# Modulation units in pairs, with the first two dense units accumulated between them

## The reference, cut to what matters

```
m  = silu(cond) @ w_ada + b_ada          # 6 * 2048 wide, for two conditions
sh1, sc1, g1, sh2, sc2, g2 = split(m, 6)
h  = rmsnorm(x, n1g) * (1 + sc1) + sh1   # pre-norm and modulation
u  = h @ w_in                            # one wide input projection: GLU | q | k | v | gates
```

## Time and profile before

| | |
|---|---|
| median of 3 runs | 3283.35 us (3283.23 to 3284.37) |
| profiled execution, its own time | 3287.09 us |
| profiled execution, span of the trace | 3285.5 us |
| granted TensorE clock, mean | 0.965 |
| TensorE matmul busy | 3072.2 us, 94% of the span |
| VectorE busy | 1935.6 us, 59% |
| ScalarE busy | 1391.3 us, 42% |
| read from HBM | 681.60 MB |

### The profile page before, as it was taken

One profiled execution on the slowest core, in us unless ns is written; L12 is line 12 of the kernel. 1 busy time (PEld: TensorE's weight loads), 2 busy tenths in 40 slices (PEclk: granted clock), 3 DMA queues, 4 the chain that ended last, 5 costly groups with the idle time before them and its releaser, 6 DMA issues.

```text
span 3285.5 us, 52731 instructions
## 1 busy us (share of the span) xinstructions
PE 3072.2 (94%) x20582; PEld 2612.3 (80%) x20582; DVE 1935.6 (59%) x1988; ACT 1391.3 (42%) x1669; POOL 278.1 (8%) x438
## 2 busy tenths in 40 slices
PE   5599999999999899989999999599999999999995
PEld 4499999999989898979999999466666666666663
DVE  4323332136556465657325333599999989999894
ACT  2311111124333342433312122277777777777774
POOL 0011110001100100111001111100000000000000
PEclk7699999999999999999999999799999999999997
DMA  8533332224534444454334533599999999999994
GB/s 356 208 113 118 119 123 100 77 89 156 191 140 153 183 157 178 162 188 143 126 133 169 165 125 118 213 345 390 388 390 379 374 382 390 385 383 378 374 388 136
DMA packets 123892, 745.97 MB, mean 227 GB/s; under 512 B 16592, under 2 KB 26896, under 8 KB 43968
## 3 DMA queue, kind: packets, MB, share of 16 engines
q1 hardware_dynamic: 96368, 631.28, 49.8%
q0 software_dynamic: 27376, 112.60, 11.0%
HBM read 681.60 MB, written 55.66 MB: 224 GB/s over the span
## 4 chain that ended last, share of the span: by engine, by line
PE 76%; DVE 9%; issue 5%; ACT 3%; DMA 2%; DVEq 0%; SPq 0%; POOL 0%; ACTq 0%; POOLq 0%
PE pu L849 22%; PE pu L593 15%; PE pu L594 15%; PE pu L595 15%; DVE elo L1652 4%; PE pt L697 2%; PE pt L573 2%; ACT ehi L1152 2%; DVE xe L1664 1%; PE pt L685 1%; PE ps L667 1%; DVE wlo L1229 1%; PE ps L675 1%; ACT whi L882 1%; DMA att<-att 1%
## 5 line engine op out<-in xcount | busy, mean ns | idle before, releaser
L593 PE MATMUL pu<-hhi,whi 128*128 128x320 f32 x3328 | 1048.0, 315 | 49.8 <-DVE wlo L1229 32.1
L594 PE MATMUL pu<-hlo,whi 128*128 128x320 f32 x3328 | 1032.8, 310 | 1.4 <-issue 1.4
L595 PE MATMUL pu<-hhi,wlo 128*128 128x320 f32 x3328 | 1032.4, 310 | 0.0
L1652 DVE TENSOR_TENSOR elo<-ering,ehi 128x2048 fp32r<-128x2048 f32 x384 | 874.9, 2288 | 107.1 <-ACT ehi L1152 103.9
L1152 ACT CAST ehi<-ering 128x2048 fp32r<-128x2048 f32 x384 | 731.5, 1912 | 238.3 <-PE pu L849 238.1
L593 PEld LDWEIGHTS pu<-hhi,whi 128*128 128x128 f32 x3328 | 629.5, 189 | 51.9 <-issue 46.3
L594 PEld LDWEIGHTS pu<-hlo,whi 128*128 128x128 f32 x3328 | 629.3, 189 | 3.9 <-issue 2.1
L595 PEld LDWEIGHTS pu<-hhi,wlo 128*128 128x128 f32 x3328 | 628.6, 189 | 0.0
L1229 DVE TENSOR_TENSOR wlo<-raw,whi 128x2048 fp32r<-128x2048 f32 x112 | 256.6, 2291 | 291.5 <-ACT whi L882 290.7
L882 ACT CAST whi<-raw 128x2048 fp32r<-128x2048 f32 x112 | 213.0, 1902 | 503.4 <-PE pu L595 463.3
L849 PE MATMUL pu<-ehi,xhi 128*80 128x512 f32 x1024 | 322.0, 395 | 2.1
(11 more groups left out here) (262 smaller groups left out, 2836.9 us busy)
## 6 DMA issues: line engine op xcount, KB each, us to landing
ering<-in_w_experts SPq DMA_DIRECT2D x384, 1024.0 KB, 8.3
raw<-in_w_ada SPq DMA_DIRECT2D x96, 1024.0 KB, 7.2
raw<-in_w_in SPq DMA_DIRECT2D x72, 1024.0 KB, 4.9
raw<-in_w_attn_out SPq DMA_DIRECT2D x16, 1024.0 KB, 5.2
raw<-in_w_out SPq DMA_DIRECT2D x16, 1024.0 KB, 4.9
gates_tanh<-th POOLq DMA_DIRECT2D x32, 320.0 KB, 2.4
gl<-gates_tanh POOLq DMA_DIRECT2D x32, 320.0 KB, 3.5
raw<-in_w_conv_out SPq DMA_DIRECT2D x8, 1024.0 KB, 4.9
```

The lines of the kernel that those rows point to most:

```text
L593: nc.tensor.matmul(o, whi[:, dk, w:w + 128], hi[:, kt, cols], start=kt == 0, stop=False)
L594: nc.tensor.matmul(o, whi[:, dk, w:w + 128], lo[:, kt, cols], start=False, stop=False)
L595: last = nc.tensor.matmul(o, wlo[:, dk, w:w + 128], hi[:, kt, cols], start=False, stop=kt == kts - 1)
L1652: nc.vector.tensor_tensor(elo[:, j % AHEAD, :], ering[:, slot, :], ehi[:, j % AHEAD, :].bitcast(F32), ALU.subtract).then_inc(ex_lo, 1)
```

## The change

- **Loads.** SP loads the conditions and the four pieces of x first, then modulation units 0 and 1, then dense units 0 and 1 into slots 2 and 3, then the other 30 modulation units. POOL keeps five small inputs.
- **Order of the modulation units.** They alternate, shift 0, scale 0, shift 1, scale 1 and so on (`ada_of`), in two PSUM banks of `pt` and with two row buffers; a unit's fold is now issued inside the unit after it.
- **Norm first.** TensorE sums over channels before any modulation unit. ScalarE does the root after the read-out of unit 2, and the splits of dense units 0 and 1 right behind it; VectorE does their low parts right behind the norm.
- **Tile by tile.** As soon as a pair has given shift and scale of tile kt, VectorE makes the scaled tile (product with `rstd`, `gsc`, 1271, 1273), ScalarE copies it to `hhi`, and VectorE subtracts for `hlo`. ScalarE's own scale and shift is gone.
- **Dense units 0 and 1 in between.** After modulation units 5, 7, ..., 31 TensorE issues the 12 matmuls of one channel tile for dense units 0 and 1 (`first_units`), into four PSUM banks of `pu`; tiles 14 and 15 follow the last fold. The loop over dense units then has only unit 0's transposes left to do for d = 1, and goes on with d = 2.

```diff
+def ada_use(j):
+    return raw_use(j if j < 2 else j + 2, 0, 1, 0, 0)
+def ada_of(j):
+    return j // 2 + (KT if j % 2 else 0)
...
# sync_program
+        sp.dma_start(cond[:, :, :], a["cond"]).then_inc(cond_loaded, 16)
+        for c in range(4):
+            sp.dma_start(xin[:, 4 * c:4 * c + 4, :], a["x"][:, 4 * c:4 * c + 4, :]).then_inc(x_loaded[c], 16)
+        for j in range(A1):
+            load(a["w_ada"][ada_of(j)], *ada_use(j), first=j < 2)
+            if j == 1:
+                for d in range(2):
+                    load(a["w_in"][d], 2 + d, 0, first=True)
...
# tensor_program
+        pe.wait_ge(fold_made, 1)
         pe.wait_ge(sq_summed, KT)
         mean_over_channels(t1, ps, HALF, norm_mm)
...
+        def first_units(kt):
+            for d in range(2):
+                if kt == 0:
+                    dense_start(d, d)
+                pe.wait_ge(h_hi, kt + 1)
+                pe.wait_ge(h_lo, kt + 1)
+                dense(d, d, d, d, hhi, hlo, kt, kt + 1, 0, KT)
+
+        rows = (row0, row1)
+        for j in range(A1):
+            ada_unit(*ada_use(j), j - 1 if j > 1 else None, pt[:, j % 2, :], rows[(j + 1) % 2][:, :] if j else None,
+                     j if j else None)
+            if j >= 5 and j % 2:
+                first_units((j - 5) // 2)
+        pe.wait_ge(ada_read, A1)
+        row_out(pt[:, 0, :], row1[:, :]).then_inc(ada_turned, 1)
+        for kt in (KT - 2, KT - 1):
+            first_units(kt)
...
# scalar_program
+        def modulated_hi(kt):
+            act.wait_ge(xn_ready, kt + 1)
+            nc.scalar.copy(hhi[:, kt, :], xin[:, kt, :]).then_inc(h_hi, 1)
+        for j in range(A1):
+            ada_read_out(*ada_use(j), ada_of(j - 1) if j else None, pt[:, j % 2, :], rows[j % 2][:, :])
+            if j == 2:
+                act.wait_ge(norm_t, 2)
+                nc.scalar.activation(rstd[:, :], t2[:, :], ACT.Sqrt).then_inc(norm_sq, 1)
+                for d in range(2):
+                    split_hi(2 + d, 0, d, d)
+            if j >= 3 and j % 2:
+                modulated_hi((j - 3) // 2)
         act.wait_ge(ada_turned, 1)
+        add_bias(ada_of(A1 - 1), pt[:, 0, :]).then_inc(mod_ready, 1)
+        modulated_hi(KT - 1)
...
# vector_program
+        for d in range(2):
+            split_lo(2 + d, 0, d, d)
...
         for kt in range(KT):
+            link(nc.vector.tensor_tensor(xin[:, kt, :], xin[:, kt, :], rstd[:, :], ALU.mult))
+            if kt < KT - 1:
+                vec.wait_ge(ada_read, 2 * kt + 3)
+            else:
+                vec.wait_ge(mod_ready, 1)
+            link(nc.vector.scalar_tensor_tensor(out=gsc[:, kt, :], in0=mod[:, KT + kt, :], scalar=1.0,
+                                                in1=norms[:, 0, kt, :], op0=ALU.add, op1=ALU.mult))
...
+            vec.wait_ge(h_hi, kt + 1)
             nc.vector.tensor_tensor(hlo[:, kt, :], xin[:, kt, :], hhi[:, kt, :].bitcast(F32),
                                     ALU.subtract).then_inc(h_lo, 1)
```

More of the change, by code:

```diff
@@ L117, in build @@
     fold, o = at("fold", [128, 2], F32, o)
-    row4, _ = at("row4", [128, RAW, 128], F32, X0)
+    row0, _ = at("row0", [128, 128], F32, SMALL - 512 - KT * 128 - 512)
     row1, _ = at("row1", [128, 128], F32, SMALL - 512)
@@ L128, in build @@
     rstd, o = at("rstd", [128, N], F32, o)
-    assert o <= SMALL - 512 - KT * 128
+    assert o <= SMALL - 512 - KT * 128 - 512
     zt, o = at("zt", [128, CT, ZW], F32, Y0)
@@ L248, in build @@
     x_loaded = [sem(f"x_loaded{i}") for i in range(4)]
+    cond_loaded = sem("cond_loaded")
     const_made, fold_made = sem("const_made"), sem("fold_made")
@@ L253, in build @@
     vec_done = sem("vec_done")
-    gsc_ready = sem("gsc_ready")
     xn_ready = sem("xn_ready")
@@ L320, in load @@
             sp.dma_start(raw[:, slot, :], src).then_inc(raw_loaded[slot], 16)
[L322 to L327, removed]
+        sp.dma_start(cond[:, :, :], a["cond"]).then_inc(cond_loaded, 16)
[6 more added lines that the diff above has]
+                    load(a["w_in"][d], 2 + d, 0, first=True)
+        for d in (2, 3):
+            load(a["w_in"][d], *raw_use(G_Q, 1, U, 0, d))
+        with sp.Fori(1, (QN + GN) // U) as i:
             for k in range(U):
@@ L384, in pool_program @@
                            pattern=[[-1, 128]], channel_multiplier=1).then_inc(const_made, 1)
-        for dst, name in ((cond, "cond"), (bada, "b_ada"), (norms, "norms"), (taps, "taps"), (convp, "convp"),
+        for dst, name in ((bada, "b_ada"), (norms, "norms"), (taps, "taps"), (convp, "convp"),
                           (sinks, "sinks")):
             pool.dma_start(dst[:], a[name]).then_inc(small_loaded, 16)
-        for c in range(4):
-            pool.dma_start(xin[:, 4 * c:4 * c + 4, :], a["x"][:, 4 * c:4 * c + 4, :]).then_inc(x_loaded[c], 16)
         pool.wait_ge(h_lo, KT)
@@ L563, in tensor_program, with ada_unit @@
     def tensor_program(pe):
-        def ada_unit(slot, use, read, bank, row):
+        def ada_unit(slot, use, read, bank, row, row_read=None):
             pe.wait_ge(raw_loaded[slot], 16 * (use + 1))
-            pe.wait_ge(ada_read, read)
+            if read is not None:
+                pe.wait_ge(ada_read, read)
             for kt in range(KT):
@@ L575, in ada_unit @@
             if row is not None:
+                if row_read is not None:
+                    pe.wait_ge(ada_read, row_read)
                 last = row_out(bank, row)
@@ L617, in tensor_program @@
         pe.wait_ge(cond_ready, 1)
-        for k in range(RAW):
-            ada_unit(*raw_use(0, 1, RAW, 0, k), k + 1, pu[:, k, :], None)
+        pe.wait_ge(fold_made, 1)
         pe.wait_ge(sq_summed, KT)
         mean_over_channels(t1, ps, HALF, norm_mm)
[L623 to L640, removed]
+        def first_units(kt):
[15 more added lines that the diff above has]
+            first_units(kt)
+        for d in range(1, 2 * NKV):
+            if d >= 2:
+                dense_start(d, d)
+                dense(d, d, d % 2, d % 2, hhi, hlo, 0, KT, 0, KT)
+            if d <= NKV:
                 n = d - 1
@@ L725, in tensor_program @@
                         ada_unit(at_ % RAW, at_ // RAW + i * (3 * US // RAW),
-                                 i * (2 * US) + (RAW + A1 + 2 * k + x), pt[:, 1, :], row1[:, :])
+                                 i * (2 * US) + (A1 + 2 * k + x), pt[:, 1, :], row1[:, :])
                     else:
@@ L732, in tensor_program @@
                         pv(i, n)
-        pe.wait_ge(ada_read, RAW + ADA)
+        pe.wait_ge(ada_read, ADA)
         row_out(pt[:, 1, :], row1[:, :]).then_inc(ada_turned, 1)
@@ L898, in ada_read_out @@
             last.then_inc(ada_read, 1)
-        act.sem_inc(ada_read, RAW)
         for freed in (att_exp, att_pt, att_out):
             act.sem_inc(freed, 1)
-        act.wait_ge(small_loaded, 16 * 6)
         act.wait_ge(const_made, 4)
+        act.wait_ge(cond_loaded, 16)
         nc.scalar.activation(cond32[:, :, 0:2], cond[:, :, :], ACT.Silu).then_inc(cond_ready, 1)
@@ L910, in scalar_program @@
             nc.scalar.activation((t2 if kt % 2 else t3)[:, :], xin[:, kt, :], ACT.Square).then_inc(sq_made, 1)
[L911 to L919, removed]
-        act.wait_ge(ada_turned, 1)
[L921 to L930, removed]
+        act.wait_ge(small_loaded, 16 * 5)
+        def modulated_hi(kt):
+            act.wait_ge(xn_ready, kt + 1)
+            nc.scalar.copy(hhi[:, kt, :], xin[:, kt, :]).then_inc(h_hi, 1)
+        rows = (row0, row1)
+        for j in range(A1):
[7 more added lines that the diff above has]
+                modulated_hi((j - 3) // 2)
+        act.wait_ge(ada_turned, 1)
+        add_bias(ada_of(A1 - 1), pt[:, 0, :]).then_inc(mod_ready, 1)
+        modulated_hi(KT - 1)
         def ahead(i, k, body, first, stride, d0, count, nxt):
@@ L941, in scalar_program @@
         scalar_program.ahead = ahead
-        act.wait_ge(h_lo, KT)
-        for d in range(2):
-            split_hi(*raw_use(G_Q, 1, U, 0, d), d, d % 2)
         for d in range(2 * NKV):
@@ L1259, in vector_program @@
         link(nc.vector.tensor_tensor(rstd[:, :], rstd[:, :], t3[:, :], ALU.mult))
+        for d in range(2):
+            split_lo(2 + d, 0, d, d)
+        vec.wait_ge(small_loaded, 16 * 5)
+        nc.vector.tensor_scalar(negsink[:, :], sinks[:, :], -1.0, None, ALU.mult)
         for kt in range(KT):
[L1261 to L1270, removed]
+            link(nc.vector.tensor_tensor(xin[:, kt, :], xin[:, kt, :], rstd[:, :], ALU.mult))
[5 more added lines that the diff above has]
+                                                in1=norms[:, 0, kt, :], op0=ALU.add, op1=ALU.mult))
             nc.vector.tensor_scalar(xin[:, kt, 0:NL], xin[:, kt, 0:NL], gsc[:, kt, 0:1], mod[:, kt, 0:1],
                                     ALU.mult, ALU.add)
-            link(nc.vector.tensor_scalar(xin[:, kt, NL:N], xin[:, kt, NL:N], gsc[:, kt, 1:2], mod[:, kt, 1:2],
-                                         ALU.mult, ALU.add))
```

(5 more changed lines are left out.)

## The result

The changed kernel takes 3242.16 us (median of 4, 3241.31 to 3244.30), the one before 3283.86 beside it (3283.23 to 3286.18). The ratio is 0.9875, 95% interval 0.9864 to 0.9887: 41.7 us or 1.25% less. The forecast was 3244.8, 38.6 us less. One execution of the kernel before (7353.03 us) and one of the last experiment's kernel (7804.12 us) took more than twice as long as the others of their kernel and are left out of every median and ratio.

The account below looks back on a forecast made before the run. Loads, then 67 us nearly without data, were taken to bound the front before dense unit 2. Stream 118.5 + stalls 2 + tail 13.5 + low clock 2 = 136.0 against 174.6: 38.6 us less, 3244.8 us, range 3232 to 3262.

Parts of the forecast that it names:

- What bounds the front: Before dense unit 2: loads until 107 us, then 67 us with nearly no data; its start at 174.60 decides the time.
- The front up to unit 4: Norm's sum, unit 2, root, dense unit 0's splits, then unit 4's load at 44.6 and unit 4 at 51.1 us.
- the first load after a hole: From issue of a load after an idle DMA to its unit's start on TensorE: 6.5 us.
- The 27 units to unit 31: Modulation stream from unit 4 to unit 31: 2.50 us a unit, 67.4 us, so unit 31 at 118.5.
- The table load: ScalarE's load ahead of the norm's root, now on the path: priced at 1.28 us, without 1.38 us of drain.
- TensorE keeps up: Between 51 and 118 us: a pair takes 4.43 us of 4.99, 89%, mostly at the high clock.
- The 2 us charged for stalls: In the modulation stream: 2 us lost to stalls after stretches of TensorE at the low clock.
- The first rival: TensorE's clock is low half the time between units: 5.75 us a pair, 3253.5 us; chance 0.17.
- low throughout: TensorE's clock stays low all through the stream: 8.2 us a pair, 3288 us; chance 0.05.
- slower: TensorE low and each unit waits for ScalarE's read-out of the one before: 9.3 us a pair, 3303 us; chance 0.05.
- The overlap isn't had: In the stream, slots are freed late or tiles pile up behind it: 23 us more, 3267 us; chance 0.10.
- The tail: From unit 31 to dense unit 2: last tiles, then splits, 13.5 us; 2 us more for the low clock.

Follow-up runs that it names:

- the last experiment's kernel: ScalarE copies tile 0 behind unit 4's read-out instead of unit 3's, against the kernel holding dense unit 1's tiles 10 to 15 back: 3233.93 us, 0.9852.
- the second run: The changed kernel run once more with nothing changed, beside the kernel before on another chip: 3241.82 us, 0.9874.

## Why the prediction was right, point by point

**What bounds the front.** Right. Dense unit 2's start moved 43.8 us and the medians 41.7; taking the tiles out of the stream gave 22.6 back.

**The front up to unit 4.** Each link was right. The sum started at 23.0 (forecast 23.3), unit 2 at 32.3 (33.9), the root at 36.5 (38.3), unit 4's load at 42.75 (44.6), unit 4 at 47.5 (51.1). The term that was mis-sized is the first load after a hole: I took 6.5 us from 43.30 to 49.78, and it was 4.8 here (42.75 to 47.54), 4.7 and 4.9 in the second run and with the root earlier. The 27 units to unit 31 took 70.1 us and not 67.4. The two together were 73.9 by the forecast and 74.9 measured, and unit 31 came at 117.6 for 118.5. That it came so near is partly luck, as unit 4 was 3.6 us too early and the stream 2.7 us too long. Why the row's load took 6.5 us isn't shown.

**The table load.** The root starts at 36.50, 0.02 us after the 1.28 us of the load, and at 30.87 behind one that began at 29.57. The row's price was right. One reading was not: before, the load ran from 38.45 to 39.73, during the norm's sum, and the reciprocal began at 42.27; nothing in the sum hangs on it. The Trainium skill, ScalarE: Activation LUTs, section "What ACT_TABLE_LOAD costs", adds 1.38 us of drain; the trace doesn't agree, no such time lies ahead of the load or behind it.

**TensorE keeps up.** Right: 91% busy for 89, mean clock 0.98. The 2 us charged for stalls weren't lost. They and the stream's 0.9 are most of the 3 us by which the forecast was too careful. The first rival is refuted: low half the time it would have shown near 0.75, and even at 0.69 the stream lost nothing where the tiles lay outside. By the Trainium skill, TensorE: Matmul & The Clock Gate, section "A second HAM failure mode: psum-queue depth-cycling", this rival was the likeliest; the trace doesn't agree, as a TensorE that goes round six banks stayed at 0.98, and round four at 1.00. The rivals "low throughout" and "slower" fall with it; the read-outs of 0.54 us were hidden by the matmuls before the fold.

**The overlap isn't had.** Refuted: 91% busy with the DMA at 1.01.

**The tail.** Right to 0.3 us: dense unit 2 13.2 us after unit 31 (13.5), a wait of 1.4 us for the last tile and 3.7 for the splits, and 2.5 us at the low clock for the 2 charged. In every run in which a gap of 3.68 us stands before dense unit 2 the clock is low behind it, but when and how long varies. In the first run with the dense loads behind unit 3 the first four matmuls came 0.15 us apart, and the low stretch lasted from 124.3 to 127.6 us; in the changed kernel's second run it lasted from 128.9 to 132.2, in its first from 130.8 to 136.4. That is some 12 to 21 matmuls, 1.4 to 2.5 us. No run here shows what sets the length.

## What to carry to other kernels

When a stretch is bound by loads and the next by compute, ask what of the next can be done on the part that has landed: here 23 us of matmuls and the whole elementwise work went under a stream that took no longer for it. A ring loaded in one order makes every slot's release a condition for all later loads, so put ahead only what is freed soon: two dense units that waited for the norm's root cost a hole of 10 us, and two positions later in the same order brought 7.9 back. A hole that is closed shows the next one; follow a late unit, not the GB/s, and look at what stands before it on its engine as well as at its load.

## What the runs showed of the hardware

TensorE's clock went by more than its busy share: 78% busy with modulation units alone had a mean of 0.69, 75% with one dense unit's tiles among them 1.00. After the tail's wait the clock fell in every run, to 0.50 for 3 to 6 us, and holding tiles back to fill the wait moved the low stretch and didn't remove it. A load of 1 MB issued after a hole reached TensorE 4.7 to 4.9 us later, while the 23 modulation loads issued between 52 and 117 us, in the full stream, took 8.3 us from issue to landing in the median: the loads behind others took longer, and the last one of the stream too, 9.0 us.
